# The first feed-forward block of a two-block transformer by one Strassen level, with its gates kept in HBM

## The reference, cut to what matters

```python
def conv_ffn(h, w_in, conv_w, conv_b, w_out):          # D_FF = 2816
    u, v = jnp.split(h @ w_in, 2, axis=-1)
    u = conv(u, conv_w, 3 taps, causal, one filter per feature) + conv_b
    return (jax.nn.gelu(u, approximate=False) * v) @ w_out
# first block
x = x + gt_m * y                                       # y: the attention's output product
h = rmsnorm(x, g_ffn) * (1 + sc_f) + sh_f
x = x + gt_f * conv_ffn(h, ...)
x = rmsnorm(x, g_final)
# second block: f = square(relu(u @ w_ff1)) @ w_ff2, D_FF_2 = 4096, and so on
```

## Time and profile before

| what | from, to (us) | PE busy | DVE busy | POOL busy | DMA share |
|---|---|---|---|---|---|
| first block's output product | 559.6 to 651.6 | 90.70 | 54.48 | 42.25 | 0.41 |
| first feed-forward block | 651.6 to 1389.4 | 733.67 | 319.59 | 162.76 | 0.13 |
| second feed-forward block, first units | 1787.6 to 1841.7 | 45.57 | 44.12 | 23.97 | 0.49 |
| its early matrices | 1841.7 to 1951.5 | 108.00 | 105.84 | 13.95 | 0.54 |
| its late matrices | 1951.5 to 2106.0 | 154.50 | 123.63 | 29.73 | 0.47 |
| its last down group | 2284.0 to 2401.0 | 115.86 | 99.15 | 0.00 | 0.33 |

### The profile page before, as it was taken

The page is one execution under the profiler, slowest core; times in us unless marked ns, Lnnn a source line. Parts: engine busy times, 40 slices in busy tenths (PEclk is TensorE's granted clock), DMA queues, the critical chain, the costliest instruction groups (busy, mean ns, idle before and its releaser), DMA issues. The chain is left out here.

```text
span 2456.1 us, 30997 instructions
## 1 busy us (share of the span) xinstructions
PE 2300.6 (94%) x11293; PEld 1947.3 (79%) x11293; DVE 1549.3 (63%) x2482; ACT 1017.3 (41%) x1692; POOL 487.9 (20%) x418
## 2 busy tenths in 40 slices
PE   8989699989999999999999998978989999999996
PEld 5779688877888888888888888957878788788875
DVE  7699666656544334344433857465489977757797
ACT  5478555444321211212121546176554333554441
POOL 2021122114232212122221211111430122000002
PEclk9975599999999999999999999989999999999997
DMA  9024100005211111111111010001255544854431
GB/s 371 18 78 154 56 20 10 26 1 172 86 52 52 40 46 50 44 51 51 51 34 52 26 35 26 18 18 52 80 189 183 206 150 157 309 163 144 152 95 69
DMA packets 71329, 220.37 MB, mean 90 GB/s; under 512 B 8720, under 2 KB 12976, under 8 KB 68784
## 3 DMA queue, kind: packets, MB, share of 16 engines
q1 hardware_dynamic: 66752, 190.32, 22.8%
q10 hardware_dynamic: 4464, 28.58, 2.8%
HBM read 178.24 MB, written 40.63 MB: 89 GB/s over the span
## 5 line engine op out<-in xcount | busy, mean ns | idle before, releaser
L1979 ACT CAST w_hi<-w_raw 128x512 fp32r<-128x512 f32 x152 | 94.1, 622 | 230.1 <-PE set L160 99.2
L158 PE MATMUL set<-gate_hi,w_hi 128*128 128x512 f32 x420 | 164.6, 392 | 3.3 <-issue 2.6
L3454 DVE TENSOR_SCALAR work<-work,vec 128x1024 f32<-128x1024 f32 x22 | 17.9, 813 | 236.0 <-ACT work L3184 228.9
L160 PE MATMUL set<-gate_hi,w_lo 128*128 128x512 f32 x420 | 164.3, 391 | 0.0
L159 PE MATMUL set<-gate_lo,w_hi 128*128 128x512 f32 x420 | 164.3, 391 | 0.0
L3476 DVE SCALAR_TENSOR_TENSOR x<-down,mod,x 128x512 f32<-128x512 f32 x160 | 120.0, 750 | 66.4 <-PE down L160 64.4
L158 PE MATMUL set<-b_hi,w_hi 128*128 128x512 f32 x384 | 151.1, 393 | 5.8 <-DVE w_lo L2309 5.8
L159 PE MATMUL set<-b_lo,w_hi 128*128 128x512 f32 x384 | 150.6, 392 | 0.0
L160 PE MATMUL set<-b_hi,w_lo 128*128 128x512 f32 x384 | 150.6, 392 | 0.0
L158 PE MATMUL v_ps<-z_hi,ffn_v_hi 128*128 128x512 f32 x336 | 133.0, 396 | 0.0
L158 PE MATMUL u_ps<-z_hi,ffn_u_hi 128*128 128x512 f32 x336 | 133.0, 396 | 0.0
(11 more groups left out here) (568 smaller groups left out, 6519.8 us busy)
## 6 DMA issues: line engine op xcount, KB each, us to landing
w_raw<-in_w_ff SPq DMA_DIRECT2D x53, 512.0 KB, 3.8
gate_raw<-gates SPq DMA_DIRECT2D x105, 256.0 KB, 2.8
gates<-x ACTq DMA_DIRECT2D x15, 1536.0 KB, 5.7
ada<-in_ada_w SPq DMA_DIRECT2D x32, 512.0 KB, 3.3
work<-in_f_w_u SPq DMA_DIRECT2D x22, 512.0 KB, 3.4
work<-in_f_w_v SPq DMA_DIRECT2D x22, 512.0 KB, 3.6
work<-in_f_w_out SPq DMA_DIRECT2D x22, 512.0 KB, 4.3
down_raw<-in_w_ff SPq DMA_DIRECT2D x18, 512.0 KB, 5.0
```

What stands on the lines that cost most here:

```text
L158: nc.tensor.matmul(out, w_hi, x_hi, start=start, stop=False)
L160: return nc.tensor.matmul(out, w_lo, x_hi, start=False, stop=stop)
L1979: nc.scalar.copy(w_parts(n)[0][:, :], source(n)).then_inc(w_hi_s, 1)
L3454: nc.vector.tensor_scalar(conv, u, w(2), bias, ALU.mult, ALU.add).then_inc(conv_s, 1)
```

## The change

`middle` is rewritten after the pattern of `mixer_out_ffn`. u and v are 11 matrices each (two feature tiles), in turn: 22 matrices by 7 units in the up phase, 10 pairs by 7 units in two groups of 3 and 7 pairs in the down phase, in which the kinds have an order of their own, and the last pair plain. `Units` takes sizes, order and the unit up to which GpSimd makes the low parts of the raw kinds (P1, P2, P4) as arguments; for `mixer_out_ffn` they are what they were (4, 5, 6; the old order; the up phase), and nothing else changes there.

```diff
-SIZES = (4, 5, 6)
+SIZES_1, SIZES_2 = (3, 7), (4, 5, 6)
+DOWN_1 = (P1, P2, P7, P6, P4, P5, P3)
+DOWN_2 = (P1, P2, P7, P6, P5, P3, P4)
@@ class Units
     def on_pool(self, n):
-        return n < self.first_down and self.all[n][1] in RAW_KIND
+        return n < self.pool_until and self.all[n][1] in RAW_KIND
@@ middle
+    MATS = 2 * PAIRS
+    units = Units(MATS, SIZES_1, DOWN_1, 7 * MATS)
```

TensorE, before and after, behind the 16 output products:

```diff
-                for h, n in enumerate("uv"):
-                    products(n, 1, o_hi[h], o_lo[h])
-                pair(0, 0, True)
-                with pe.Fori(0, (PAIRS - 3) // 2) as i:
...
-                for h in range(2):
-                    pe.wait_ge(o_lo_s[h], PAIRS)
-                pe.wait_ge(g_lo_s, FF1)
+                early_product(0, 0, HALF)
+                sum_squares(1)
+                early_product(1, 0, 2)
+                spread(1)
+                early_product(1, 2, HALF)
+                for n in range(2, 2 * EARLY):
+                    early_product(n, 0, HALF)
+                for n in range(2 * EARLY, UP):
+                    up_unit(n)
+                for n in range(UP, ALL):
+                    down_unit(n)
+                pe.wait_ge(end_lo_s, 4)
                 for m in range(N):
                     last_down(m)
```

```diff
+                def keep_x(n):
+                    a, k = n // KT, n % KT
+                    sp.wait_ge(x_s, n + 1)
+                    sp.dma_start(d["x_keep"][k][:, span[a]], tok(k, a)).then_inc(kept[a], 16)
...
                 def scale(a, k):
...
                     dve.wait_ge(spread_s, a + 1)
+                    dve.wait_ge(kept[a], 16 * KT)
```

In the up phase VectorE's iteration is that of the second block; the convolution and the gates are spread over the iterations of the next matrix (`conv_start` and `gelu_row` are ScalarE's, of 1024 columns; `conv_tap` is a STT of 1023 or 1022 columns, `gate11` to `gate12` and `sum1` to `sum4` are of 512):

```diff
+                def finish_u(x, i):
+                    early = 2 * x < EARLY
+                    if x and i == (P7 if early else P1):
+                        gate21(x - 1)
+                        sum3(x - 1)
+                    if x and i == (P6 if early else P2):
+                        sum2(x - 1)
+                    if x and i == (P5 if early else P7):
+                        sum4(x - 1)
+                    if i == P4:
+                        conv_tap(x, 0, 1)
+                def finish_v(x, i):
+                    early = 2 * x < EARLY
+                    if i == (P7 if early else P1):
+                        conv_tap(x, 0, 2)
+                    if i == (P7 if early else P2):
+                        conv_tap(x, 1, 1)
+                    if i == (P6 if early else P7):
+                        conv_tap(x, 1, 2)
+                    if i == P6 and not early:
+                        gate11(x)
+                    if i == P3:
+                        gate22(x)
+                    if i == P4:
+                        gate12(x)
```

In the down phase ScalarE copies the sets of P1, P7, P6 and P5 of the first group to SBUF; VectorE adds those of the second group to them (`add_sum`), joins them as Winograd's form asks (`join`), and multiplies each result by its gate column and adds it to x (`fold`, 512 columns, 40 in all; P2, P4 and P3 straight from PSUM). SyncE's queue in the first down units:

```diff
+                for b in range(4, len(units.down)):
+                    load_gate(b)
+                    if b == 4:
+                        bring_x(0)
+                    if b == 5:
+                        for f in range(2):
+                            load_down(1, 0, f)
+                    if b == 6:
+                        bring_x(1)
+                    if b in (7, 8):
+                        sp.wait_ge(done, UP)
+                        for f in range(2):
+                            load_down(1, b - 6, f)
+                    if b in (9, 10, 11):
+                        sp.wait_ge(conv_s, 4 * PAIRS)
+                        for f in range(2):
+                            load_down(1, b - 6, f)
+                    if b in (12, 14):
+                        bring_x(b // 2 - 4)
```

More of the change, by code:

```diff
@@ L1355, in __init__ @@
                 self.place[n_up + first + j] = (q, j)
-            self.down += [(n_up + p, i) for i in range(7) for p in self.pairs[-1]]
+            self.down += [(n_up + p, i) for i in down_order for p in self.pairs[-1]]
             first += size
@@ L2662, in middle @@
+def middle(c, d, work, xs, mixer, places, wo_raw):
     nc = c.nc
@@ L2664, in middle @@
     LAST, PER = PAIRS - 1, T2 // CH2
[L2665 to L2669 removed]
+    MATS = 2 * PAIRS
+    units = Units(MATS, SIZES_1, DOWN_1, 7 * MATS)
+    UP, ALL = units.first_down, len(units.all)
     q_hi, q_lo = (c.sb(mixer, n, [P, 4, T2], F32R) for n in ("q_hi", "q_lo"))
     c.sb(mixer, "mixer_pad", [P, 32])
+    lru = RecurrentTiles(places)
@@ new lines, in middle @@
+        decay, up8, soft = (pl.small[n] for n in ("decay", "up8", "soft"))
+        lam_t = [pl.small[f"lam{i}"] for i in range(4)]
+        banks = c.ps(st, "banks", [P, 8, 512])
+        sets = [banks[:, 0:4, :], banks[:, 4:8, :]]
+        mix = [banks[:, 4:7, :], banks[:, 1:4, :]]
+        gate = [banks[:, 7, :], banks[:, 0, :]]
+        bank = lambda n: banks[:, n % 4, :]
+        ring = lambda m: banks[:, m % 4, :]
+        SPREAD = [banks[:, 4, :], banks[:, 5, :]]
+        TOTALS = banks[:, 7, :]
@@ new lines, in _ @@
+                sp.wait_ge(pool_lo, units.low[5])
+                load_early(6)
+                keep_p2(2)
+                sp.wait_ge(pool_lo, units.low[7])
+                load_early(7)
+                sp.wait_ge(pool_lo, units.low[9])
+                load_up(1, 1)
+                sp.wait_ge(pool_lo, units.low[11])
+                load_up(0, 0)
+                for w in range(3, 6):
+                    keep_p2(w)
+                sp.wait_ge(pool_lo, units.low[13])
+                load_up(0, 1)
@@ new lines, in down_unit @@
+                def down_unit(n):
+                    w, i = units.all[n]
+                    b, s = n - UP, units.step(n)
+                    (q, j), g = units.place[w], b % 4
+                    hi, lo = w_parts(n)
+                    if j == 0:
+                        set_free(s)
+                    low_done(pe, n)
+                    pe.wait_ge(gate_lo_s, b + 1)
+                    for t in range(HALF):
+                        mm = three_products(nc, sets[s % 2][:, t, :], hi[:, col4[t]], lo[:, col4[t]], gate_hi[g][:, :],
+                                            gate_lo[g][:, :], j == 0, j == SIZES_1[q] - 1)
+                    mm.then_inc(done, 1)
@@ L3195, in pair, with first_high @@
-                def pair(p, odd, last=False):
-                    for h in range(2):
-                        step(p * 2 + 2 + h, 2 * (1 - odd) + h, not (last and h))
-                        act.wait_ge(down_s, p * N + KT * (h + 1))
-                        weights_o(p + 1, h)
+                def first_high(k):
+                    act.wait_ge(scaled_s, scaled_count(0, k))
+                    if k >= HALF:
+                        act.wait_ge(pool_lo, 2)
+                    nc.scalar.activation(b_hi[k // HALF][:, k % HALF, :], tok(k, 0), ACT.Identity,
+                                         bias=c.mod[:, SH_F + k:SH_F + k + 1]).then_inc(h_hi_s, 1)
@@ L3536, in _ @@
-                pair(LAST - 1, 1)
+                for kk in range(HALF):
+                    scale(1, kk)
+                    scale(1, HALF + kk)
+                for kk in range(HALF):
+                    t3_full(kk)
+                    t2_full(kk)
+                for kk in range(HALF):
+                    part_low(P7, 0, kk)
+                for kk in range(HALF):
+                    t4_full(kk)
+                for kk in range(HALF):
+                    part_low(P6, 4, kk)
+                for kk in range(HALF):
+                    difference(kk)
@@ new lines, in _ @@
+                weights_low(18)
+                weights_sum(19)
+                for n in range(17, ALL):
+                    if n - 1 < UP:
+                        unit_out(*units.all[n - 1])
+                    w, i = units.all[n]
+                    if n + 2 < UP:
+                        if not units.on_pool(n + 2):
+                            weights_low(n + 2)
+                        if n + 3 in units.combined:
+                            weights_sum(n + 3)
+                        if n + 3 == UP:
+                            gate_low(0)
+                    else:
+                        if n + 3 in units.combined:
+                            weights_sum(n + 3)
+                        if n + 3 < ALL:
+                            gate_low(n + 3 - UP)
+                        if n + 2 < ALL:
+                            weights_low(n + 2)
+                    if n - 1 < UP:
+                        before, kind = units.all[n - 1]
+                        (finish_v if before % 2 else finish_u)(before // 2, kind)
+                    if n >= UP:
+                        q, j = units.place[w]
+                        s = units.step(n)
+                        if j == 0 and 1 <= s <= 7 and DOWN_1[s - 1] in FOLDS_1:
+                            fold_set(0, DOWN_1[s - 1])
+                        if q == 1:
+                            last_group(i, j)
@@ L3668, in _ @@
                 u_low(N - 1)
+                lambdas()
                 for i in range(2 * N):
```

1308 lines of the change are left out of this document (897 added, 411 removed).

## The result

The changed kernel takes 2377.19 us (median of 4 runs, 2377.15 to 2377.78) against 2457.96 us for the kernel before in the same series (4 runs, 2455.79 to 2460.84): ratio 0.9671, 95% interval 0.9659 to 0.9684, 80.8 us less. The forecast was 2364, with a range of 2354 to 2388: the direction and the range held, and the change brought 13 us less than forecast. The profiled execution took 2377.8 us with a span of 2375.9.

The account below looks back on a forecast made before the run. TensorE's matmul count was taken as the bound: 631.1 us of matmuls plus small matmuls and stalls made 646.1 for the block's 737.8; with 1.7 saved ahead, 2364 us. Own range 2354 to 2374; with two rivals, 2354 to 2388.

Parts of the forecast that it names:

- ahead of the block: packed tiles: The 384 matmuls of the output products before the block read packed tiles too: 1.7 us less.
- small matmuls among them: Ones and identity matmuls between the block's products stay as they are: 2 us in all.
- (a): Start of the block, first 16 units covering the making of other operand sums: 1.5 us lost, ends 0 and 12.
- (b): Other 40 units of the eight early matrices: TensorE waits 7 us for VectorE's work, ends 0 and 14.
- (c): The 14 late matrices of the up phase, VectorE at 89%: 1 us lost, ends 0 and 6.
- (d): Up to down, 10 MB in SyncE's queue during the first 14 down units: 1 us lost, ends 0 and 3.
- (e): Second down group of 7 pairs, VectorE at 87%: 1 us lost, ends 0 and 4.
- (f): End of the block: the hole before the last pair's down products goes, VectorE's folds and additions cost 0 us.
- unit borders: Allowance for unseen losses at the block's 224 unit borders: 1.5 us.
- The second block's stops at the start: Rival: the block's start repeats these stops with their half clock, 10.5 us more, 2375; chance 0.10.
- the rival with VectorE as the bound of the early part: Early part bound by VectorE with taps at their lengthened mean: 15 us more, 2380; chance 0.22.
- my signs of being wrong: Up pitch of 0.231, waits in late units, or granted clock falling inside the block; no last-pair hole was expected.

Follow-up runs that it names:

- p2_narrow_taps: Changed kernel with the second and third convolution taps cut to 16 columns for the first eight matrices (work left out): 2372.66 us, ratio 0.9643.
- m1_meta_early: Changed kernel with ScalarE squaring the meta columns before it turns to the block's first weights: 2374.82 us, ratio 0.9666.
- m6_meta_and_x: Changed kernel with the meta squares first on ScalarE and the three later quarters of x requested behind gate blocks 12, 14 and 17: 2369.03 us, ratio 0.9638.
- p3_pool_p3_too: Changed kernel with GpSimd also making the low parts of the P3 units in the first eight matrices: 2379.00 us, ratio 0.9677.
- m5_x_behind_weights: Changed kernel with the three later quarters of x requested behind gate blocks 12, 14 and 17 in SyncE's queue: 2372.56 us, ratio 0.9646.
- m3_mix_later: Changed kernel with GpSimd's first two low parts for the next stage moved behind the first of the last additions: 2376.13 us, ratio 0.9674.

## Why the prediction was right, and where it was off

| step of the prediction | forecast, us | measured, us |
|---|---|---|
| ahead of the block: packed tiles | -1.7 | +2.0, and +1.2 before the stage |
| 2784 matmuls at 0.2267 | 631.1 | 631.1, no other pitch |
| small matmuls among them | 2 | 1.8 |
| (a), (b), (c): up phase | 1.5, 7, 1 | 1.8, 6.6, 0 |
| (d) up to down | 1 | 6.8 (4.5 to 6 in five other executions) |
| (e) second down group | 1 | 0.7 |
| (f) last pair | 0 | 5.4 |
| unit borders | 1.5 | nothing seen |

**What held.** The block was bound by how many matmuls TensorE has to run. By the measured paces the change takes 98.3 us of matmuls away (264 x 0.2320 + 120 x 0.2267 + 1848 x 0.0053), and 83.3 arrived; the other 15.0 are stops and half clock, of which the block before had 8.4 us and this one has 23.4. That the pitch of the second block would come with the packed tiles held too; my 18 starts in the earlier trace rows gave 0.231 where the mean is 0.2320, so the pitch accounts for 1848 x 0.0053 = 9.8 us of the gain and not 8, which changes nothing in a sum made at 0.2267. (b) is the step that I worked out longest, and p2_narrow_taps shows its mechanism, VectorE's load: the up phase is 6.7 us shorter without the taps' work. That its 7 us came out is in part luck: the stops themselves are 4.2 us and the half clock behind one of them 1.7, where I had only pieces of under a microsecond and no loss of clock. In m1_meta_early and m6_meta_and_x two stops of 2.65 us stand there and no half clock. The second block's stops at the start did not come back, and the late matrices lost nothing. The whole up phase, 429.3 us, is 1 us under my sum for it (430.4), so the rival with VectorE as the bound of the early part at 15 us more is not what happened, though its 2380 lies nearer to the measured time than my 2364. The 0.5 us that (b) took for a meeting of VectorE and GpSimd is what the groups show as a mean too: 5.1 us over ten operations.

The Trainium skill ("SBUF — State Buffer", section "SBUF: two separate sides") was weighed for (b): a VectorE instruction with two SBUF inputs and a GpSimd instruction that reads SBUF exclude each other for the whole length of one. The runs agree: 0.29 us became 2.19, operations that read PSUM kept their 0.75, and handing GpSimd more work made the up phase 3.2 us longer (p3_pool_p3_too).

**Where (d) failed.** I priced bytes: 1.25 MB per unit at 410 GB/s, covered by four gate blocks asked for ahead. The wait for the last spill I named only in passing. And I took four blocks asked for ahead as 10.9 us of cover. m5_x_behind_weights has the whole 6.8 us back with the wait and 1 MB gone from this place. What decides is when the awaited transfer is issued (1088.03, by ScalarE behind the last Gelu), how long it takes among others, and that a request needed every 2.72 us is queued behind. Against the 10.9 us the queue stood for 10.4, and the block's own transfer took six more (1095.86 to 1101.80). Even without the wait a block needed 5 to 11 us from request to landing in m5, which eats the cover nearly up.

The slower rate that the Trainium skill gives from HBM ("SBUF — State Buffer", section "A bandwidth-pool intuition that's wrong"), about 358 GB/s, would have made it worse than it is: 412 GB/s ran here with TensorE fully busy.

**Where (f) failed.** I let the hole of the earlier trace rows go and costed what comes after at nothing, by VectorE's operations at their bare lengths. The timeline of the kernel before has GpSimd's two low parts for the next stage right behind the one in the earlier trace rows:

```profile
1365.84 2.36 POOL L2848 TENSOR_TENSOR ffn_u_lo<-work,ffn_u_hi 128x1024 fp32r<-128x1024 f32 x1
1368.16 2.38 POOL L2848 TENSOR_TENSOR ffn_v_lo<-work,ffn_v_hi 128x1024 fp32r<-128x1024 f32 x1
```

VectorE's first addition there starts at 1368.92 after 5.50 us of idleness, waiting for TensorE, so they met hardly anything. The stop that the change removes was their cover. In the changed kernel they fall on the last folds, 4 x 1.05 = 4.2 us for VectorE, and a stop of 3.72 us with 1.6 at half clock is there again, in another place. m3_mix_later shows that cause (folds at 0.68), and also that it is not the whole 5.4 us: with the folds short the last pair still took 3.0 us more than its matmuls, 2.8 of them the stops beside the operations of VectorE that GpSimd's two then lengthened. No free place for them was found in the two that were tried. So two of my signs of being wrong did show: the hole in the last pair stayed, and the granted clock fell inside the block, for some seven matmuls at a time.

**Ahead of the block.** I took the output product as unchanged but for its tiles and did not follow ScalarE's queue through it. ScalarE's operation on the meta columns now stands behind two casts that wait for loads (4.29 and 3.54 us) and a square that waits for x (2.92), and came 7.6 us later (578.38 for 570.77). TensorE stopped 2.26 us and lost 1.4 at half clock; m1_meta_early takes back all of it. The 1.2 us before the stage lie in code that is the same in both; other runs of these kernels start it up to 2.7 us earlier.

**A slip in the working.** The upper end of (b), by its own terms (38 by 0.69 and 1 us per meeting), comes to 18 us and not 14, so the sum of all upper ends to 2396; the range did not use it.

## What to carry to other kernels

For each transfer that the engine on the path needs at a steady pace, look at what its queue does just ahead of it: a request that must wait for another engine's late transfer holds back everything behind it, and requests made ahead cover only what is left after their own landing time at the full rate. When a stall is removed, list what the other engines did during it, since that work lands on something else. And a share of VectorE's work is worth giving to GpSimd where VectorE reads PSUM or idles; beside operations with two SBUF inputs the share here cost about what it saved (5.1 of 6.1 us in two groups).

## What was new about the hardware

- Beside a GpSimd operation of 2.4 us, VectorE's operation of 128x128 took 2.19 us instead of 0.29, and a 128x512 one 2.24 instead of 0.74; the addition between them, which reads PSUM, kept 0.74.
- A matmul of 512 columns out of rows 4176 bytes apart that begin at byte 64 takes 0.2320 us, out of one row 0.2303, from byte 0 of it 0.2290 (0.2262 and 0.2274 for one tile, 0.2342 for the other), out of packed tiles 0.2267.
- A stop of 3.56 us cost half clock in one execution of the last pair (granted clock 0.94), and one of 3.57 us none in another (m6_meta_and_x, 1.00). Of 32 stops of 2.1 to 3.6 us idle between 565 and 1312 us in the eleven traces of the changed kernel and its edits, 23 were followed by 5 to 13 matmuls at half clock, 0.2 us more each, and 9 by none. So an edit that removes such a stop wins its length, and up to 2.6 us more by chance.
